# Sample-token attention scores issued in two halves around a third of a projection, and six unread matmuls at the end of the attention phase

## The chip, the cores and the metric

The kernel runs on one core of a Trainium2 chip. The metric is the device time of one launch in microseconds (us); the median of the runs of the kernel before is 1272.56 us.

## What is computed

One layer of a decoder trunk for 1024 prompt tokens and 64 sample tokens (8 sequences of 8), model width 1024. Cut to what matters here:

```python
xn = rmsnorm(x, norm_attn_g)
a, b, q, k, v, ga, gb = split(xn @ w_in)             # a, b, ga, gb: 1024 columns each
glu = a * sigmoid(b)
conv_out = silu(layernorm(causal_depthwise_conv(glu, w_dw, width=31))) @ w_conv_out
s = q @ k.T / 8 + rel_bias;  p = softmax([s, sink])   # window of 128, 16 heads, 4 kv heads
attn_out = (p @ v) @ w_attn_out                        # sample tokens: 128 cached keys + 8 new
h = x + (sigmoid(ga) * conv_out + sigmoid(gb) * attn_out) @ w_out
y = h + hier_moe(rmsnorm(h))                           # top group, then 2 of its 8 experts
```

## The kernel before

Every large product is done as three float16 products (high by high, high by low, low by high: the helper `mm3`, lines 74 to 76), so its operands are cut into a high half by ScalarE and a low half by VectorE. The program has three phases, each a block in which the five engines run their own instruction streams and wait for each other on semaphores: `attention_phase` (q, k, v and the attention of the prompt tokens), `conv_phase` (the projections a, b, ga, gb, the convolution, and the attention of the sample tokens), `ffn_phase` (output projection, routing, experts). Between phases all engines meet (line 96 ends a block; `phase_end` clears the semaphores on GpSimd, line 2718, and has the engines meet again, line 2720).

The order in each engine's stream is written by hand. What bears on the change:

- **End of the attention phase.** TensorE's last work is `feature(16, 24)`, the last third of the first b projection (bank `c_psb`). Its last product raises `feat_mm`, which VectorE waits for at the end of its own block. The helper `keep_warm` (line 743) issues products of 512 columns into the bank `a_psP` that nobody reads; `last_tile` uses it in three places.
- **A product of `conv_phase`** (`product`) computes 128 output features for all 1092 token columns in three thirds of 364 columns, 24 products of 0.15 us each. The a projections go to the bank `c_psa`, b and ga to `c_psb`. `first_chunk` on TensorE goes: 20 small transposes of the sample q and k (`sample_turn`, lines 1593 and 1596), the a projection (product 1), `sample_scores` for four groups of heads (lines 1612, 1616, tiles of 32 columns), product 2 (ga) with the transposes of the sample probabilities (`sample_turn_probs`, line 1624) ahead of its last third, `sample_turn_new` (line 1631), product 3 with `sample_values` (1644, 1648) and `sample_turn_out` (1655) between its thirds.
- **Scores.** The four groups share two halves of the bank `c_psm`: group 2 overwrites group 0, so TensorE waits for VectorE's logits of groups 0 and 1 (`s_logit`).
- **VectorE** in the same stretch: the low halves of the sample operands and of two weight chunks (lines 1312 to 1326, 1288), then `chunk(0, 0)`, the gated product a times sigmoid(b) (lines 1301, 1304, waits through ScalarE's line 1072 for all of product 1), then `sample_softmax`, which begins with the logits of the four groups (line 1334, two a group) and ends in two small operations on the maxima (1341, 1345), then the weight cut `low(4, 0)` (1288), then `conv`: 29 taps of about 1.2 us (line 1396) into which other work is put by count. After the tap of j = 8 stand the low halves of the transposed probabilities (`sample_probs`, line 1360), after j = 10 those of the new keys' (1367).
- **ScalarE**: `glu_a` (1072), the first tap (1078), the weight cut `cut(4, 0)` (1062), the second tap (1087), eight exponentials of the sample softmax (1139), further cuts, the high halves of the transposed probabilities (1147).

`sample_turn_probs` waits for all eight exponentials (`s_exp`); `sample_turn_new` waits, bank half by bank half, for the low halves of line 1360 (`s_pT_low`), because it overwrites them.

Of the kernel before, what the change touches and what calls it, by code (L numbers as in the profile page):

```python
# [36 lines left out]
HD, NH, NKV = 64, 16, 4  # L37
# [34 lines left out]
def mm3(pe, out, stat, mov, start, stop):  # L72

    pe.matmul(out, stat[0], mov[0], start=start, stop=False)  # L74
    pe.matmul(out, stat[0], mov[1], start=False, stop=False)  # L75
    return pe.matmul(out, stat[1], mov[0], start=False, stop=stop)  # L76
# [17 lines left out]
def attention_phase(nc, sem, g, A):  # L94

    with ExitStack() as c:
# [524 lines left out]
        def _(pe):  # L621
# [146 lines left out]
            def feature(first, last):  # L768

                for i in range(first, last):  # L770
                    third, k = i // KC, i % KC
                    cols = slice(third * THIRD, (third + 1) * THIRD)
                    done = mm3(pe, g.psb[:, third, 0:THIRD], (g.f_w_h[:, 0, k], g.f_w_l[0][:, k]),
                               (g.xnT_h[:, k, cols], g.xnT_l[:, k, cols]), k == 0, k == KC - 1)
                if last == 3 * KC:
                    done.then_inc(feat_mm, 1)
# [63 lines left out]
            last.then_inc(T_done, 1)  # L840
            pe.wait_ge(s_free, 16 * NT)
            feature(16, 24)


def conv_phase(nc, sem, g, A):
# [3 lines left out]
    with ExitStack() as c:  # L849
# [39 lines left out]
        def take32(n):  # L889
# [24 lines left out]
        s_q_low, s_kn_low, s_kT_low, s_v_low, s_vn_low = (sem("s_" + n) for n in (  # L914
            "q_low", "kn_low", "kT_low", "v_low", "vn_low"))
# [51 lines left out]
        def slot32(n):  # L967
            if isinstance(n, int):
                return w32[:, n % W32]
            return w32[:, ds(n % W32, 1)].rearrange("p a n -> p (a n)")  # L970
# [308 lines left out]
        def _(dve):  # L1279
# [6 lines left out]
            def low(n, pos):  # L1286
                dve.wait_ge(w_high, n + 1)
                dve.scalar_tensor_tensor(w_l[pos], slot32(n).rearrange("p (k m) -> p k m", k=KC), S_W,
                                         w_h[:, pos], op0=ALU.mult, op1=ALU.subtract).then_inc(w_low, 1)
# [7 lines left out]
            def chunk(k, p):  # L1297
                dve.wait_ge(th_done, k + 1)
                dve.wait_ge(a_out, k + 1)
                dve.wait_ge(hist_ld, 16 * k + 16)  # L1300
                dve.scalar_tensor_tensor(glu[:, p, HIST:HIST + SEQ], th[:, 0:SEQ], 1.0, a_s[:, 0:SEQ],
                                         op0=ALU.add, op1=ALU.mult).then_inc(glu_done, 1)
                seqs = glu[:, p, HIST + SEQ:].rearrange("p (b n) -> p b n", b=NSEQ)
                dve.scalar_tensor_tensor(seqs[:, :, HIST:], th[:, SEQ:T].rearrange("p (b i) -> p b i", b=NSEQ), 1.0,  # L1304
                                         a_s[:, SEQ:T].rearrange("p (b i) -> p b i", b=NSEQ),
                                         op0=ALU.add, op1=ALU.mult).then_inc(glu_done, 1)
# [19 lines left out]
                    dve.scalar_tensor_tensor(s_vn_l[:, h], g.v_s[HS * h:HS * h + HS, :], S_X, s_vn_h[:, h],  # L1326
                                             op0=ALU.mult, op1=ALU.subtract).then_inc(s_vn_low, 1)

            def sample_softmax():
                for grp in range(NKV):  # L1330
                    dve.wait_ge(s_mm, grp + 1)
                    for h in range(2):
                        u = 2 * grp + h
                        dve.tensor_tensor_reduce(s_p[:, u], ps_s[:, grp % 2, h], g.s_bias[:, grp], scale=1.0 / S_LOGIT,
                                                 scalar=NEG, op0=ALU.add, op1=ALU.max,
                                                 accum_out=s_st[:, 0, u:u + 1]).then_inc(s_logit, 1)
                dve.wait_ge(s_logit, SU)
                dve.sem_inc(s_stat, 1)
                dve.wait_ge(s_sink, 1)
                sink_b = g.s_nsink[:].unsqueeze(2).to_broadcast([P, NKV, 2])  # L1340
                dve.scalar_tensor_tensor(s_st[:, 1].rearrange("p (g h) -> p g h", h=2),
                                         s_st[:, 0].rearrange("p (g h) -> p g h", h=2), -1.0, sink_b, op0=ALU.mult,
                                         op1=ALU.min).then_inc(s_stat, 1)
                dve.wait_ge(s_stat, 2)
                dve.tensor_tensor(s_st[:, 2].rearrange("p (g h) -> p g h", h=2),
                                  s_st[:, 1].rearrange("p (g h) -> p g h", h=2), sink_b, ALU.subtract).then_inc(s_stat, 1)
                dve.memset(y[:, :, T:TM], 0.0).then_inc(setup, 1)
                dve.wait_ge(vec_ld, 16)
                dve.tensor_scalar(halves[:], vecs[:, 1:3], 0.5, None, ALU.mult).then_inc(setup, 1)
# [70 lines left out]

            sample_operands()
            low(3, 3)
            chunk(0, 0)
            sample_softmax()
            low(4, 0)
            dve.wait_ge(taps_ld, 16)
# [118 lines left out]
        def _(pe):  # L1545
# [41 lines left out]
            def half(j):  # L1587
                return slice(HD * (j // 2), HD * (j // 2) + HD)

            def sample_turn():  # L1590
                for h in range(NH):
                    out = ps_q[:, h // 8].rearrange("d b (h i) -> d b h i", h=8)[:, :, h % 8]
                    last = pe.transpose(out, g.q_s[0:TS, h * HD:(h + 1) * HD], g.ident[0:TS, 0:TS])
                last.then_inc(s_q_mm, 1)
                for grp in range(NKV):
                    last = pe.transpose(ps_k[:, grp // 2, grp % 2], g.k_s[0:TS, grp * HD:(grp + 1) * HD], g.ident[0:TS, 0:TS])
                last.then_inc(s_k_mm, 1)

            def sample_scores():
                pe.wait_ge(s_q_low, 2)  # L1600
                pe.wait_ge(s_kn_low, 2)
                pe.wait_ge(s_kT_low, 1)
                for grp in range(NKV):
                    r, heads = half(grp), slice(32 * (grp % 2), 32 * (grp % 2) + 32)
                    if grp > 1:
                        pe.wait_ge(s_logit, 2 * (grp - 1))
                    for h in range(2):
                        out = ps_s[:, grp % 2, h]
                        for i, (q, k) in enumerate(((s_qT_h, s_kT_h), (s_qT_h, s_kT_l), (s_qT_l, s_kT_h))):
                            for b4 in range(4):  # L1610
                                b = 4 * h + b4
                                pe.matmul(out[32 * b4:32 * b4 + 32, 0:WIN], q[r, b, heads],
                                          k[r, (grp % 2) * NSEQ + b, :], start=i == 0, stop=i == 2)
                        for i, (q, k) in enumerate(((s_qT_h, s_kn_h), (s_qT_h, s_kn_l), (s_qT_l, s_kn_h))):
                            for b4 in range(4):
                                last = pe.matmul(out[32 * b4:32 * b4 + 32, WIN:SW], q[r, 4 * h + b4, heads],
                                                 k[r, grp % 2, HS * h:HS * h + HS], start=i == 0, stop=i == 2)
                    last.then_inc(s_mm, 1)

            def sample_turn_probs():  # L1620
                pe.wait_ge(s_exp, SU)
                for bank in range(2):
                    for i in range(4):
                        last = pe.transpose(ps_t[:, bank, i], s_p[:, 4 * bank + i, 0:WIN], g.ident[:])
                    last.then_inc(s_pT_mm, 1)
# [32 lines left out]
            def keep_warm(n, bank, from_):  # L1658
                for i in range(n):
                    pe.matmul(bank, from_[:, i % KC, 0:P], from_[:, i % KC, 0:512], start=True, stop=True)  # L1660

            def first_chunk():
                pe.sem_inc(b_mm, 1)
                sample_turn()
                product(1, 1, psa, a_mm, xn, (0, 1))
                pe.wait_ge(s_kn_low, 2)
                product(1, 1, psa, a_mm, xn, (2,))
                sample_scores()
                pe.wait_ge(th_done, 1)
                product(2, 2, psb, ga_mm, xn, (0, 1))  # L1670
                sample_turn_probs()
                product(2, 2, psb, ga_mm, xn, (2,))
                sample_turn_new()
                pe.wait_ge(a_out, 1)
                product(3, 3, psa, ex_mm, xn, (0,))
                sample_values()
                product(3, 3, psa, ex_mm, xn, (1,))
                sample_turn_out()
                product(3, 3, psa, ex_mm, xn, (2,))

            def chunk(u, p, first=False):
# [14 lines left out]
                product(4 * k + 3, 3, psa, ex_mm, o if p else xn)  # L1696

            first_chunk()
            chunk(0, 1, True)
            with pe.Fori(1, KC // 2) as u:  # L1700
# [1153 lines left out]
```

## Time and profile before

| | |
|---|---|
| time, three runs | 1270.76, 1272.56, 1273.21 us (median 1272.56) |
| the profiled execution | 1273.04 us, of which the span of the trace 1271.4 us |
| TensorE busy | 1228.9 us (97%) |
| VectorE, ScalarE, GpSimd busy | 1036.4, 705.8, 311.5 us |
| mean granted clock of TensorE | 0.994 of full speed |
| attention phase, conv phase, ffn phase on TensorE | to 291.2, 292.8 to 842.6, from 843.9 us |

Times in the rows are us from the start of the span. A row of a timeline tells when an instruction (or a run of like ones) began and how long it lasted, and in brackets how long its engine had been idle before it and who ended that. Matmuls overlap in the pipe: a product of 364 columns is shown with 0.32 us but a new one begins every 0.15 us. A granted clock of 1.00 is 2.4 GHz, 0.50 is 1.2 GHz.

### The profile page before, as it was taken

To read this page: it belongs to the slowest core of one execution; us is meant where nothing else is said; L and a number is where in the kernel's file an instruction comes from. 1 tells how busy PE (TensorE), PEld (TensorE's weight loads), DVE (VectorE), ACT (ScalarE), POOL (GpSimd) and SP (SyncE) were. 2 spreads that over 40 slices of the span, in tenths; PEclk is the share of its full clock that TensorE was granted. 3 is DMA by queue.
4 is the path that set the end of the run, shared out by engine and by line. 5 is a ranking of instruction groups with operands and counts; after the bars stand their busy time and mean duration, and the time that the engine had idled before them with its cause. 6 is when DMAs were issued, how large, how long until landed. Compare 5 with 4: busy or idle time off the path is not lost. (4 is left out here: it accounts for less than half of the span.)

```text
span 1271.4 us, 28372 instructions
## 1 busy us (share of the span) xinstructions
PE 1228.9 (97%) x11174; PEld 821.8 (65%) x11174; DVE 1036.4 (82%) x1479; ACT 705.8 (56%) x1160; POOL 311.5 (25%) x280
## 2 busy tenths in 40 slices
PE   7899999998999999999999999999998999999995
PEld 5456666665666666666665666655555888888884
DVE  5777777776989999999999676535756999999993
ACT  5656666666443452354343664423222899999983
POOL 1383111111010010011000000000134367667663
PEclk9999999998999999999999999999999999999998
DMA  9700000033141442244141145547678999999982
GB/s 349 173 10 3 1 0 0 3 122 101 56 110 54 125 111 76 84 127 110 36 137 51 52 143 202 173 172 278 235 235 307 321 391 386 391 398 384 387 307 48
DMA packets 53081, 211.34 MB, mean 166 GB/s; under 512 B 14560, under 2 KB 15776, under 8 KB 40416
## 3 DMA queue, kind: packets, MB, share of 16 engines
q1 hardware_dynamic: 31888, 156.95, 33.1%
q0 software_dynamic: 18672, 44.42, 14.4%
q10 hardware_dynamic: 2448, 8.98, 1.8%
q8 instruction: 47, 0.77, 0.3%
q14 instruction: 26, 0.21, 0.1%
HBM read 180.98 MB, written 39.72 MB: 174 GB/s over the span
## 5 line engine op out<-in xcount | busy, mean ns | idle before, releaser
L1396 DVE SCALAR_TENSOR_TENSOR big<-c_region,c_taps,big 128x1024 f32<-128x1024 f32 (+1 forms) x120 | 153.4, 1279 | 3.7 <-ACT caT L1087 3.7
L74 PE MATMUL c_psb<-xnT,w_taken 128*128 128x364 f16 x456 | 145.5, 319 | 0.0
L75 PE MATMUL c_psb<-xnT,w_taken 128*128 128x364 f16 x456 | 145.5, 319 | 0.0
L1396 DVE SCALAR_TENSOR_TENSOR caT<-c_region,c_taps,caT 128x1024 f32<-128x1024 f32 x112 | 143.2, 1278 | 0.0
L2095 POOL DMA_INDIRECT y_all<-o_hn,e_idx_y x29 | 91.9, 3168 | 38.8 <-POOL e_idx_y L2091 23.3
L74 PE MATMUL c_psa<-xnT,w_taken 128*128 128x364 f16 x312 | 99.8, 320 | 0.1
L75 PE MATMUL c_psa<-xnT,w_taken 128*128 128x364 f16 x312 | 99.8, 320 | 0.0
L74 PE MATMUL o_psH<-big,e_gu 128*128 128x128 f16 x512 | 87.4, 219 | 0.8 <-DVE big L2442 0.8
L75 PE MATMUL o_psH<-big,e_gu 128*128 128x128 f16 x512 | 87.4, 219 | 0.0
L76 PE MATMUL o_psH<-big,e_gu 128*128 128x128 f16 x512 | 87.4, 219 | 0.0
L76 PE MATMUL c_psb<-xnT,f_w_l_first 128*128 128x364 f16 x240 | 76.2, 317 | 0.0
L353 ACT ACTIVATE big<-big,a_ntop 128x256 f32<-128x256 f32 (+1 forms) x128 | 61.4, 483 | 20.5 <-DVE a_ntop L505 20.5
L270 POOL TENSOR_TENSOR a_rs<-a_ms,neg_half 128x20 f32<-128x20 f32 x9 | 31.8, 3539 | 160.2 <-DVE a_ms L461 160.2
L76 PE MATMUL c_psb<-xnT,f_w_l 128*128 128x364 f16 x216 | 69.2, 320 | 0.0
L2431 DVE SCALAR_TENSOR_TENSOR e_gu<-e_gu 128x2048 f16<-128x2048 f32 x28 | 64.0, 2289 | 5.5 <-ACT e_gu L2157 5.5
L1018 POOL DMA_DIRECT2D sc_prompt<-c_region x8 | 4.6, 573 | 260.4 <-DVE c_region L1304 260.4
L74 PE MATMUL a_psP<-big,xnT 128*128 128x512 f16 x176 | 66.9, 380 | 0.0
L75 PE MATMUL a_psP<-w_taken,xnT 128*128 128x512 f16 x176 | 66.7, 379 | 0.0
L76 PE MATMUL a_psP<-big,xnT 128*128 128x512 f16 x176 | 66.7, 379 | 0.0
L74 PE MATMUL c_psa<-oT_h,w_taken 128*128 128x364 f16 x192 | 61.0, 318 | 1.2 <-ACT c_gate_b L1116 1.2
L76 PE MATMUL c_psa<-xnT,f_w_l_first 128*128 128x364 f16 x192 | 61.6, 321 | 0.0
L74 PEld LDWEIGHTS c_psb<-xnT,w_taken 128*128 128x128 f16 x456 | 44.9, 98 | 25.7 <-issue 0.3
(437 smaller groups left out, 3977.2 us busy)
## 6 DMA issues: line engine op xcount, KB each, us to landing
e_gu<-w_gu SPq DMA_DIRECT2D x28, 1024.0 KB, 12.0
w_taken<-w_feat SPq DMA_DIRECT2D x48, 512.0 KB, 4.1
e_d<-w_dn SPq DMA_DIRECT2D x15, 1024.0 KB
o_room<-w_gu SPq DMA_DIRECT2D x12, 1024.0 KB
xnT<-w_gu SPq DMA_DIRECT2D x12, 1024.0 KB
big<-w_gu SPq DMA_DIRECT2D x12, 1024.0 KB
c_region<-gates POOLq DMA_DIRECT2D x8, 1092.0 KB, 5.8
xnT<-w_dn SPq DMA_DIRECT2D x6, 1024.0 KB
```

The costliest lines, as they stand in the source:

```text
L74: pe.matmul(out, stat[0], mov[0], start=start, stop=False)
L75: pe.matmul(out, stat[0], mov[1], start=False, stop=False)
L76: return pe.matmul(out, stat[1], mov[0], start=False, stop=stop)
L270: pool.tensor_tensor(rs[:], ms[:], g.neg_half[:, 0:NH + NKV], ALU.pow).then_inc(rs_done, 1)
L353: act.activation(prob[:, s, r, lo:], prob[:, s, r, lo:], ACT.Exp, bias=ntop[:, s, r:r + 1], accum_out=den[:, s, r:r + 1]).then_inc(exp_don ...
L1018: pool.dma_start(A["sc_prompt"][ds(k * P, P), :], glu[:, p, SEQ:SEQ + HIST].rearrange("p a n -> p (a n)")).then_inc(hist_ps, 16)
L1396: dve.scalar_tensor_tensor(y_j, glu[:, p, j:j + SEQ], tap, y_j, op0=ALU.mult, op1=ALU.add).then_inc(tap_done, 1)
L2095: pool.indirect_dma_start(out=A["y_all"], out_offset=bass.IndirectOffsetOnAxis(ap=idx_y[:, p:p + 1], axis=0), in_=y_o[:, p], in_offset=Non ...
L2431: dve.scalar_tensor_tensor(gu_l[:, p, halves[half]], gu32[load[0]][:, halves[half]], S_W, gu_h[:, p, halves[half]], op0=ALU.mult, op1=ALU. ...
```

## The change

TensorE scores groups 0 and 1 after two thirds of product 1, then does the last third, then scores groups 2 and 3. VectorE does the logits of groups 0 and 1 before `chunk(0, 0)` and those of groups 2 and 3 behind it. At the end of the attention phase TensorE issues six unread products of 512 columns.

```diff
@@ attention_phase, TensorE
             pe.wait_ge(s_free, 16 * NT)
             feature(16, 24)
+            keep_warm(6)
@@ conv_phase, VectorE
-            def sample_softmax():
-                for grp in range(NKV):
+            def sample_logits(groups):
+                for grp in groups:
                     dve.wait_ge(s_mm, grp + 1)
                     for h in range(2):
                         u = 2 * grp + h
                         dve.tensor_tensor_reduce(s_p[:, u], ps_s[:, grp % 2, h], g.s_bias[:, grp], scale=1.0 / S_LOGIT,
                                                  scalar=NEG, op0=ALU.add, op1=ALU.max,
                                                  accum_out=s_st[:, 0, u:u + 1]).then_inc(s_logit, 1)
+
+            def sample_softmax():
                 dve.wait_ge(s_logit, SU)
@@
             sample_operands()
             low(3, 3)
+            sample_logits((0, 1))
             chunk(0, 0)
+            sample_logits((2, 3))
             sample_softmax()
             low(4, 0)
@@ conv_phase, TensorE
-            def sample_scores():
-                pe.wait_ge(s_q_low, 2)
-                pe.wait_ge(s_kn_low, 2)
-                pe.wait_ge(s_kT_low, 1)
-                for grp in range(NKV):
+            def sample_scores(groups):
+                if 0 in groups:
+                    pe.wait_ge(s_q_low, 2)
+                    pe.wait_ge(s_kn_low, 2)
+                    pe.wait_ge(s_kT_low, 1)
+                for grp in groups:
                     r, heads = half(grp), slice(32 * (grp % 2), 32 * (grp % 2) + 32)
                     if grp > 1:
                         pe.wait_ge(s_logit, 2 * (grp - 1))
@@
                 product(1, 1, psa, a_mm, xn, (0, 1))
-                pe.wait_ge(s_kn_low, 2)
+                sample_scores((0, 1))
                 product(1, 1, psa, a_mm, xn, (2,))
-                sample_scores()
+                sample_scores((2, 3))
                 pe.wait_ge(th_done, 1)
```

The order of the instructions on VectorE around `chunk(0, 0)` (lines 1301 and 1304 before, 1302 and 1305 with the change), before:

```order
L1304 SCALAR_TENSOR_TENSOR c_region<-c_region 128x8x8
L1334 ISA caT<-c_psm,big 128x160
L1334 ISA caT 128x1
L1334 ISA caT<-c_psm,big 128x160
L1334 ISA caT 128x1
L1334 ISA caT<-c_psm,big 128x160
L1334 ISA caT 128x1
L1334 ISA caT<-c_psm,big 128x160
L1334 ISA caT 128x1
L1334 ISA caT<-c_psm,big 128x160
L1334 ISA caT 128x1
```

and with the change:

```order
L1289 SCALAR_TENSOR_TENSOR f_w_l<-w_taken 128x1024
L1335 ISA caT<-c_psm,big 128x160
L1335 ISA caT 128x1
L1335 ISA caT<-c_psm,big 128x160
L1335 ISA caT 128x1
L1335 ISA caT<-c_psm,big 128x160
L1335 ISA caT 128x1
L1335 ISA caT<-c_psm,big 128x160
L1335 ISA caT 128x1
L1302 SCALAR_TENSOR_TENSOR c_region<-c_region 128x1024
L1305 SCALAR_TENSOR_TENSOR c_region<-c_region 128x8x8
L1335 ISA caT<-c_psm,big 128x160
```

Each logit is a pair of rows. All eight pairs stood behind `chunk(0, 0)`; now four stand ahead of it and four behind. The taps and what stands between them keep their order.

On TensorE, from the end of product 1 (`c_psa`) through the scores (lines 1612 and 1616 before, 1618 and 1622 with the change) to product 2 (`c_psb`), before:

```order
L76 MATMUL c_psa<-xnT,f_w_l_first 128x364
L1612 MATMUL c_psm<-caT 32x128 x12
L1616 MATMUL c_psm<-caT 32x32 x12
L1612 MATMUL c_psm<-caT 32x128 x12
L1616 MATMUL c_psm<-caT 32x32 x12
```

and with the change, from two thirds of product 1 into its last third:

```order
L76 MATMUL c_psa<-xnT,f_w_l_first 128x364
L1618 MATMUL c_psm<-caT 32x128 x12
L1622 MATMUL c_psm<-caT 32x32 x12
L1618 MATMUL c_psm<-caT 32x128 x12
L1622 MATMUL c_psm<-caT 32x32 x12
L1618 MATMUL c_psm<-caT 32x128 x12
L1622 MATMUL c_psm<-caT 32x32 x12
L1618 MATMUL c_psm<-caT 32x128 x12
L1622 MATMUL c_psm<-caT 32x32 x12
L74 MATMUL c_psa<-xnT,w_taken 128x364
```

Eight such pairs stood behind all of product 1; four of them now stand ahead of its last third, the other four behind it.

## Rows read from the trace of the kernel before

**Rows 1.** The page, busy time and share of each engine.

```profile
PE 1228.9 (97%) x11174; PEld 821.8 (65%) x11174; DVE 1036.4 (82%) x1479; ACT 705.8 (56%) x1160; POOL 311.5 (25%) x280
```

**Rows 2.** Waits of TensorE, whole span: us in total, times, longest.

```profile
PE c_psm L1612 <- DVE caT L1334: 2.0, 1, 2.0
PE c_psm L1593 <- PEq L2720: 1.6, 1, 1.6
PE c_psm L1566 <- DVE big L1419: 0.7, 1, 0.7
```

**Rows 3.** Timeline of TensorE around the end of the attention phase.

```profile
290.88 0.32 PE L76 MATMUL c_psb<-xnT,f_w_l_first 128*128 128x364 f16 x1
...
292.79 1.05 PE L1593 MATMUL c_psm<-ident,c_gate 64*64 64x64 f32 x16 [1.59 <-PEq L2720]
...
294.00 0.47 PE L74 MATMUL c_psa<-xnT,w_taken 128*128 128x364 f16 x1
```

**Rows 4.** Windows: length, busy of each engine, TensorE's clock (third last), DMA share, GB/s.

```profile
294.00:294.10 0.10, 0.10 (x3) 0.10 (x2) 0.00 (x0) 0.10 (x1) 0.06 (x1) 0.69 0.72 248
297.40:297.50 0.10, 0.10 (x2) 0.05 (x1) 0.00 (x0) 0.10 (x1) 0.00 (x0) 0.75 0.73 246
311.10:311.20 0.10, 0.10 (x17) 0.07 (x3) 0.10 (x3) 0.10 (x1) 0.10 (x1) 0.52 0.16 29
314.50:314.60 0.10, 0.10 (x2) 0.09 (x1) 0.10 (x1) 0.10 (x1) 0.00 (x0) 0.92 0.00 0
```

**Rows 5.** Timeline of TensorE around the end of the conv phase.

```profile
839.42 3.18 PE L1660 MATMUL c_psa<-caT 128*128 128x512 f16 x14
...
843.89 0.38 PE L74 MATMUL o_psH<-xnT,big 128*128 128x512 f16 x1 [1.29 <-PEq L2720]
```

**Rows 6.** Windows around two other idle stretches of TensorE: one, and after each.

```profile
56.99:58.80 1.81, 0.00 (x1) 0.03 (x1) 1.81 (x3) 0.60 (x1) 0.00 (x0) 1.00 0.56 127
58.80:62.20 3.40, 2.36 (x14) 1.38 (x14) 3.32 (x5) 1.94 (x3) 0.00 (x0) 1.00 0.49 92
843.89:847.50 3.61, 3.61 (x17) 1.66 (x18) 0.23 (x2) 0.00 (x0) 0.15 (x1) 1.00 0.59 210
```

**Rows 7.** Timeline of TensorE around the sample scores.

```profile
306.87 0.35 PE L1612 MATMUL c_psm<-caT 64*32 64x128 f16 x12
...
310.06 0.35 PE L1612 MATMUL c_psm<-caT 64*32 64x128 f16 x12 [2.04 <-DVE caT L1334]
...
311.14 0.49 PE L74 MATMUL c_psb<-xnT,w_taken 128*128 128x364 f16 x1
```

**Rows 8.** Timeline of VectorE, from the last low half to the weight cut.

```profile
304.25 1.22 DVE L1288 SCALAR_TENSOR_TENSOR f_w_l<-w_taken 128x1024 f16<-128x1024 f32 x1
308.16 1.23 DVE L1301 SCALAR_TENSOR_TENSOR c_region<-c_region 128x1024 f32<-128x1024 f32 x1 [2.68 <-issue]
...
309.44 0.32 DVE L1334 CUSTOM_DVE_ANT_0 caT<-c_psm,big 128x160 f32<-128x160 f32 x1
...
312.39 1.22 DVE L1288 SCALAR_TENSOR_TENSOR f_w_l_first<-w_taken 128x1024 f16<-128x1024 f32 x1
```

**Rows 9.** Timeline of ScalarE: a projection out, weight cut, last exponential.

```profile
306.98 1.08 ACT L1072 ACTIVATE c_region<-c_psa 128x1092 f32<-128x1092 f32 x1 [4.62 <-PE c_psa L76]
...
310.72 1.04 ACT L1062 ACTIVATE w_taken<-w_taken 128x1024 f16<-128x1024 f32 x1
...
315.91 0.19 ACT L1139 ACTIVATION_READ_ACCUMULATOR caT<-caT 128x1 f32 x1
```

**Rows 10.** Timeline of TensorE around the last third of product 2.

```profile
320.19 1.04 PE L1624 MATMUL c_psm<-ident,caT 128*128 128x128 f32 x8
321.07 0.32 PE L74 MATMUL c_psb<-xnT,w_taken 128*128 128x364 f16 x1
...
324.77 1.04 PE L1631 MATMUL c_psm<-ident,caT 128*32 128x128 f32 x8
325.64 0.32 PE L74 MATMUL c_psa<-xnT,w_taken 128*128 128x364 f16 x1
```

**Rows 11.** Timeline of VectorE: the low halves that `sample_turn_new` waits for.

```profile
323.03 1.28 DVE L1360 SCALAR_TENSOR_TENSOR caT<-c_psm,caT 128x512 f16<-128x512 f32 x2
```

**Rows 12.** Timeline of VectorE: its wait for the second chunk.

```profile
364.48 1.22 DVE L1301 SCALAR_TENSOR_TENSOR c_region<-c_region 128x1024 f32<-128x1024 f32 x1 [4.83 <-issue]
```

## The prediction

> **What bounds the kernel now.** I read the busy shares first [rows 1]: TensorE is busy 97% of the span, so a change pays only by what it takes out of TensorE's stream, as idle time or as time at the low clock. Then the waits of TensorE [rows 2]: the longest two in the stretch of the change are 2.0 us on VectorE's logits and 1.6 us on the meeting of the engines between the phases. From the scores to the end of the convolution it has only one other, 0.7 us, on VectorE's last sum. Then the granted clock [rows 4]: it goes to 0.50 twice here, from 294.0 to 297.45 and from 311.1 to 314.5, some 3.4 us each. Half speed for 3.4 us of dense products costs 1.7 us. The first fall comes after the idle time at the phase boundary and 1.2 us of 64-column transposes [rows 3], the second after the 2.04 us of idle time between narrow score products [rows 7]. So about 2.0 + 1.6 + 1.7 + 1.7 = 7 us are at stake, and the question is how much of that the edit takes out of the path.
>
> **The six unread products.** Fourteen of them last 3.18 us, the last one 0.38 [rows 5], so one begins every 2.80 / 13 = 0.215 us, and six put TensorE's last end off by 1.29 us. Nothing hides that: VectorE's stream ends by its wait for the product just ahead of them, and all engines meet behind. What comes back: at the end of the conv phase, where such products stand last on TensorE and VectorE has finished a little before, the gap from TensorE's last end to its next start is 1.29 us [rows 5], where the boundary in question has 1.59 [rows 3], because there VectorE only begins to leave when TensorE is done. I take that 0.3 us back: **+1.0 us**, between +1.0 and +1.3. The products stand ahead of the gap, not in it: an idle stretch of about 1.3 us and the 1.2 us of transposes still follow.
>
> **The scores in halves.** Half of the scores take 311.14 - 310.06 = 1.08 us [rows 7]. The first half now stands ahead of product 1's last third, at about 303.1 (306.8 less a third of 3.7 us, the length from 321.07 to 324.77 [rows 10]). The operands are there: VectorE is past them at 304.25, where it is at the last weight cut [rows 8]. So everything that waits for the whole of product 1 comes 1.08 us later: ScalarE's line 1072 at 308.06 instead of 306.98 [rows 9], the gated product at 309.24 instead of 308.16. The four logits ahead of it cost nothing: VectorE idles 2.68 us there [rows 8], and four take about 1 us. The wait of 2.04 us is gone, as logits 0 and 1 are done by about 306.5 and TensorE wants to overwrite them at 308.06. It begins product 2 at 308.06 + 1.08 = 309.14, where it was 311.14 [rows 7], and does two thirds at full clock in 7.4 us: 316.54, against 320.19 [rows 10]. **Up to here TensorE has gained 3.65 us**, 2.0 by the wait and 1.65 by the second fall.
>
> **What is late next.** First the exponentials. They end at 316.10 [rows 9], and their chain on ScalarE begins with line 1072, so now at 317.2. TensorE stands 0.65 us, then does the transposes (0.88 us) and the last third (3.70 us) [rows 10] and is ready for `sample_turn_new` at 321.8. Second, and this decides, that step waits for the low halves that VectorE makes after its tap of j = 8 [rows 11]. VectorE's place is set by ScalarE: `cut(4, 0)` ended at 311.76 [rows 9] and now ends at 312.84, so `low(4, 0)` cannot begin at 312.39 [rows 8] but at about 312.9, 0.5 us later than before, though its logits were partly done early. All taps follow 0.5 us late. The first pair half is ready at 323.03 + 0.68 + 0.5 = 324.2, the second at 324.8. TensorE was never waiting there: it came at 324.77, 0.46 us after VectorE was done. Now it stands from 321.8 to 324.2, **2.4 us**, does four transposes, waits for the second half and goes on with product 3 at about 324.85 + 0.44 = 325.3 instead of 325.64 [rows 10]. Of the 3.65 us gained 0.35 are left. Behind it nothing else is late: the next low halves and the norm come with the taps 3 and 10 us further on, where TensorE's stream has dense thirds between, and at the second chunk VectorE has 4.83 us of slack [rows 12], so from there both go at TensorE's pace and the shift is carried to the end.
>
> Sum with the clock left aside: +1.0 - 0.35 = **+0.65 us**. The second fall is in it already (it costs 324.8 to 325.64, less than 1.7, since without it TensorE would have met the same wait on VectorE).
>
> **The clock.** Two idle stretches matter. The one at the boundary, 1.3 us idle plus 1.2 us of narrow transposes, is now 2.5 us of little work instead of 2.8. The new wait is 2.4 us between dense products. No row shows either. On one side stand 1.81 us of idle time between dense products [rows 6] and 1.29 us [rows 5, 6] after which the clock stayed at 1.00; on the other 1.59 us with transposes and 2.04 us between narrow products, which ended in a fall [rows 3, 4, 7]. Both new ones lie between, each may fall or hold. If the first holds, 1.7 us come back; if the new wait makes one, up to 1.7 us are lost, less where part of the low stretch lies in the wait itself. I take about even chances for each, so the likeliest single outcome is that one of the two falls is there: +0.65.
>
> The profiled execution took 1273.04 us, 0.5 above the median of the runs. The sum gives 1273.7 against it, 1273.2 against the median. I forecast **1273.3 us**.
>
> **Rivals.**
> 1. *Both fall* (slower). TensorE stands at `sample_turn_new`, the clock goes to half in the first third of product 3, and the one after the boundary stays: +0.65 + 1.7 = +2.35, 1274.9; with the unread products at their full 1.3 us 1275.2 (0.2% above before). For it: 2.4 us is longer than every idle stretch of this trace after which the clock held, and longer than the two before a fall. Against it: both sides of it are dense. It decides from the point where the low clock falls wholly behind the wait. The Trainium skill has a rule on its side, on the page "TensorE: Matmul & The Clock Gate", section "A second HAM failure mode: psum-queue depth-cycling": a TensorE that idles briefly between groups of matmuls again and again lets its clock swing between the levels. By that rule the two new waits would cost the clock; the trace agrees for the 2.04 us wait, not for the 1.81 us one.
> 2. *Neither falls.* The unread products carry TensorE over the boundary and the new wait is too short: +0.65 - 1.7 = -1.05, 1271.5.
> 3. *VectorE is not late.* If my placing of line 1360 is wrong, the 3.65 us stay: +1.0 - 3.65 = -2.65, 1269.9, and 1268.2 with the first fall gone as well. For it: VectorE idled 2.68 us and has work moved into that. Against it: ScalarE's chain, which sets VectorE's restart, gets later, not earlier.
> 4. *The products do not do what their name says*: the gap follows them and the clock falls as before. That is inside the forecast and rival 1.
>
> **How the numbers follow.** One of two falls 0.42, both 0.25, neither 0.20, VectorE not late 0.13. A measurement of this kernel can tell about 0.2%, 2.5 us, from no change. Slower by more than that is a good half of rival 1 and a little beside it: 0.16. Faster by more is rival 3 and the edge of rival 2: 0.15. Within: 0.69. The range leaves out most of rival 3 and the far end of rival 1: 1270.2 to 1275.6.
>
> **What would show it.** In the changed trace: line 743 six times at 291; a gap of about 1.3 us behind; product 1's last third between two halves of the scores, with no wait at either; a wait of 0.6 us before line 1630 (the transposes of the probabilities) and one of 2.4 us before line 1637 (`sample_turn_new`) on VectorE's low halves, which come 0.5 us later from the phase's start. The phase's first transpose should come 1.0 us later than before, and product 3 should begin 0.65 us later than before with one fall of the clock. No wait at line 1637 would make the prediction wrong on the fast side; any other long wait in the first chunk, or a low clock for more than 7 us in all, on the slow side.

## The result, and the profile after

22 runs of each kernel: the changed kernel 1273.93 us on the median (1271.69 to 1276.45), the kernel before 1272.64 us (1270.61 to 1276.38). The ratio is 1.0014, with a 95% interval from 1.0007 to 1.0020: 0.9 to 2.5 us slower, which is clear of zero and within 0.2%. The time was forecast at 1273.3 us. The executions of the kernel before lie in two groups, 7 at 1270.6 to 1271.4 us and 14 at 1272.2 to 1273.5 (one took 1276.4), so the 1.29 us between the medians depend on how the groups are mixed. The profiled execution of before, 1273.04 us, is of the longer kind.

The page of the profiled execution (1274.4 us) and TensorE's waits in it, in us in total, times, longest:

```profile
span 1272.8 us, 28383 instructions
PE 1229.0 (97%) x11180; PEld 821.2 (65%) x11180; DVE 1036.5 (81%) x1479; ACT 705.9 (55%) x1160; POOL 310.0 (24%) x280
```

```profile
PE c_psm L1637 <- DVE caT L1363: 2.3, 1, 2.3
PE c_psm L1598 <- PEq L2726: 1.4, 1, 1.4
PE c_psm L1630 <- ACT caT L1140: 0.6, 1, 0.6
PE c_psa L76 <- issue: 0.4, 1, 0.4
```

TensorE is as busy as before [rows 1]. The wait of 2.0 us at the scores [rows 2] is gone, and two others stand in its place: 0.6 us before the transposes of the probabilities (line 1630), on the exponentials, and 2.3 us before those of the new probabilities (line 1637), on VectorE's low halves. The last row is new at this place: 0.4 us of idle time inside product 3 that waits for nothing the profile shows ("issue").

The timeline of TensorE, where [rows 3], [rows 7] and [rows 10] were:

```profile
290.37 0.32 PE L76 MATMUL c_psb<-xnT,f_w_l_first 128*128 128x364 f16 x1
...
293.34 1.05 PE L1598 MATMUL c_psm<-ident,c_gate 64*64 64x64 f32 x16 [1.35 <-PEq L2726]
...
306.93 0.35 PE L1618 MATMUL c_psm<-caT 64*32 64x128 f16 x12
...
316.20 1.09 PE L1630 MATMUL c_psm<-ident,caT 128*128 128x128 f32 x8 [0.62 <-ACT caT L1140]
...
323.25 1.49 PE L1637 MATMUL c_psm<-ident,caT 128*32 128x128 f32 x8 [2.26 <-DVE caT L1363]
324.54 0.51 PE L74 MATMUL c_psa<-xnT,w_taken 128*128 128x364 f16 x1
```

and windows of it, TensorE's granted clock being the third number from the end:

```profile
294.00:297.50 3.50, 3.50 (x31) 2.34 (x30) 2.05 (x4) 3.37 (x6) 0.61 (x1) 1.00 0.65 137
324.00:324.50 0.50, 0.50 (x4) 0.37 (x3) 0.50 (x1) 0.49 (x1) 0.00 (x0) 0.54 0.00 0
327.00:327.50 0.50, 0.50 (x3) 0.26 (x2) 0.50 (x2) 0.00 (x0) 0.00 (x0) 0.55 0.58 227
```

Behind the boundary the clock held in this execution, and it fell once, from 324.0 to 327.3, behind the new wait. VectorE's side, in place of [rows 8] and [rows 11]: the weight cut waits for ScalarE's, and the low halves follow from it.

```profile
308.21 1.23 DVE L1302 SCALAR_TENSOR_TENSOR c_region<-c_region 128x1024 f32<-128x1024 f32 x1 [1.21 <-issue]
...
311.85 1.22 DVE L1289 SCALAR_TENSOR_TENSOR f_w_l_first<-w_taken 128x1024 f16<-128x1024 f32 x1 [0.46 <-ACT w_taken L1063]
...
322.51 1.28 DVE L1363 SCALAR_TENSOR_TENSOR caT<-c_psm,caT 128x512 f16<-128x512 f32 x2
```

Where the time went, profile against profile:

| stretch on TensorE | before | after | longer by |
|---|---|---|---|
| last useful product of the attention phase to the first transpose | 290.88 to 292.79 | 290.37 to 293.34 | +1.06 |
| to product 3 | to 325.64 | to 324.54 | -1.65 |
| first third of product 3, to the sample values | to 329.44 | to 329.77 | +1.43 |
| values and second third, to the output transposes | to 336.33 | to 337.24 | +0.58 |

Each row begins where the one above it ends. The sum is +1.42 us. The -1.65 has the fall behind the boundary in it, which before has and this execution has not. Outside of the table the attention phase was 0.51 us shorter in this execution, the way from the output transposes to the unread products at the end of the conv phase takes 503.1 us in both, and the ffn phase was 0.5 us longer, which makes up the 1.4 us between the spans.

### The profile page after: what moved, and what is told of

Its sections match the earlier page's. It is cut to its first block and busy times, and to the rows that moved or that the text cites. A ratio compares the mean times of both kernels' runs of the same rounds, so it can differ in the third digit from the quotient of the medians.

```text
span 1272.8 us, 28383 instructions
## 1 busy us (share of the span) xinstructions
PE 1229.0 (97%) x11180; PEld 821.2 (65%) x11180; DVE 1036.5 (81%) x1479; ACT 705.9 (55%) x1160; POOL 310.0 (24%) x280
```

## The experiments

They were timed beside the kernel before in three batches on three chips: e1 to e4, e5 to e8, e9 to e11. Each has a ratio to before within its batch, with a 95% interval in brackets; it comes from all executions of the two and is not the quotient of two medians. The median of before differs between the batches (1270.94, 1271.84, 1271.68 us), its mean hardly (1271.65, 1271.70, 1271.75).

For every execution of these batches the record has the mean granted clock over the span. Profiles with two falls of the clock in the first 50 us of the conv phase have 0.994 (before, e1, e8, e10), those with one 0.995 or 0.996 (after, e2, e5, e6, e11), those with none 0.996 or 0.997 (e3, e4, e7, e9). An estimate agrees: one fall costs 1.7 us of 1271, or 0.0013. Of the 90 executions of before in the batches 38 have 0.994, with a median of 1272.8 us, and 52 have more, with a median of 1270.7. So a profile is one draw out of several, and what it shows of the clock is compared with this number below.

**e1, the scores alone.**

```diff
             feature(16, 24)
-            keep_warm(6)
```

> The kernel before with the scores in halves and without the six unread products. My theory (VectorE's low halves of the probabilities decide, the scores' own gain of 3.65 us is given back at sample_turn_new): within 0.7 us of before on the median (1272.0 to 1273.3), the wait of 2.0 us at the scores gone, a wait of about 2.3 us before the transposes of the new probabilities. The rival that the halves are worth their 2 to 3.7 us and the unread products take it back: 1269 to 1270.5, no new wait.

Measured: 1272.61 us, ratio 1.0008 [0.9998, 1.0019]. TensorE's waits:

```profile
PE c_psm L1636 <- DVE caT L1362: 2.3, 1, 2.3
PE c_psm L1597 <- PEq L2725: 1.6, 1, 1.6
PE c_psm L1629 <- ACT caT L1139: 0.6, 1, 0.6
```

The halves by themselves gain nothing, and the new wait is there without the unread products. The rival that they are worth 2 to 3.7 us is out: the interval ends at a gain of 0.3 us. Its centre is 1.0 us slower, more than the 0.7 I had allowed. In this profile both falls are there, the one behind the boundary and one behind the new wait (325.1 to 328.5). From the first transpose to product 3 it takes 32.90 us against 32.85 before, and to the sample values 38.1 against 36.65.

**e2, the six products alone.** The kernel before with `keep_warm(6)` behind `feature(16, 24)`.

> The kernel before with the six unread products alone. My theory (they stand ahead of the idle stretch, lengthen the path by 1.29 us and give 0.3 back in the meeting of the engines): 1.0 us slower than before, 1273.6, where the clock falls as often as before; the gap behind them 1.3 us instead of 1.6. The rival that they keep the clock up: as fast as before or up to 0.7 us faster, with no low clock behind the boundary.

Measured: 1273.87 us, ratio 1.0015 [1.0006, 1.0024], 0.8 to 3.0 us slower.

```profile
290.40 1.46 PE L743 MATMUL a_psP<-xnT 128*128 128x512 f16 x6
293.22 1.05 PE L1594 MATMUL c_psm<-ident,c_gate 64*64 64x64 f32 x16 [1.35 <-PEq L2721]
```

The gap behind them is 1.35 us, as forecast, and they are on the path. They alone give a change of the size of the whole one. Its profile has the clock up behind the boundary and down behind the scores, and an idle time of 0.4 us on "issue" in product 3. But that execution took 1272.54 us at a mean clock of 0.995, and 7 of the 11 have 0.994, the value of profiles with two falls, with a median of 1273.9 us. So most executions of e2 seem to have one fall more than the profile; where it lies, no trace shows. The rival, as fast as before or faster, is out by the time.

**e3, the low halves two taps earlier.** The changed kernel with

```diff
-                    if first and j == 8:
+                    if first and j == 6:
                         sample_probs()
-                    if first and j == 10:
+                    if first and j == 8:
                         sample_new_probs()
```

> The changed kernel with VectorE's low halves of the probabilities after the tap j = 6 instead of 8, and those of the new keys after 8 instead of 10. My theory: the wait before the transposes of the new probabilities shrinks from 2.3 us to under 0.5, the fall of the clock behind it goes with it, 1270.5 to 1271.5 against 1273.9 of the changed kernel, so faster than before by 1 to 2 us. The rival that something else holds the first chunk (ScalarE, the second chunk's start): no change, 1273.9, with the wait turning up elsewhere.

Measured: 1270.36 us, ratio 0.9996 [0.9988, 1.0005], where the changed kernel has 1.0014. TensorE then:

```profile
315.78 1.09 PE L1630 MATMUL c_psm<-ident,caT 128*128 128x128 f32 x8 [0.63 <-ACT caT L1140]
320.44 1.21 PE L1637 MATMUL c_psm<-ident,caT 128*32 128x128 f32 x8
```

```profile
291.00:340.00 49.00, 46.62 (x664) 30.29 (x663) 42.25 (x67) 27.08 (x57) 3.37 (x4) 1.00 0.31 91
```

The wait of 2.3 us is gone, no low clock is left in the whole stretch, and the two intervals do not overlap (0.9988 to 1.0005 against 1.0007 to 1.0020), if barely, and from different batches. So the place of VectorE's low halves was what held the gain back. The time in microseconds is as forecast, but "faster than before by 1 to 2 us" is not shown: by the ratio it is 0.5 us faster, from 1.5 faster to 0.6 slower.

**e4, TensorE takes the new probabilities a third later.** The changed kernel with

```diff
-                sample_turn_new()
                 pe.wait_ge(a_out, 1)
                 product(3, 3, psa, ex_mm, xn, (0,))
-                sample_values()
+                sample_turn_new()
                 product(3, 3, psa, ex_mm, xn, (1,))
-                sample_turn_out()
+                sample_values()
                 product(3, 3, psa, ex_mm, xn, (2,))
+                sample_turn_out()
```

> The changed kernel with the transposes of the new probabilities, the sample values and the output transposes each put off by one third of product 3 on TensorE, VectorE's order untouched. My theory: TensorE has 3.7 us of products to do while VectorE makes the low halves, the wait of 2.3 us goes, 1270.5 to 1271.5. The rival that VectorE then waits for TensorE (norm after j = 14, output after j = 18) and hands the delay on: slower than that, 1272.5 or more, with idle time on VectorE ahead of lines 1377 and 1384.

Measured: 1271.84 us, ratio 1.0000 [0.9991, 1.0009]. The wait on the low halves is gone here too, and no low clock is left in the profile. VectorE waited 1.06 us for the sample values and 0.79 us at the output, but together that is no more than in after (0.6 and 1.4 us), so these waits do not speak for the rival. TensorE idled on "issue":

```profile
PE c_psm L1650 <- issue: 0.8, 1, 0.8
```

By its ratio it stands between after and e3, and its interval overlaps with both, so it is told apart from neither. Why it is above my 1271.5 stays open; in the profile product 3 ends 44.6 us behind the first transpose, as in e3.

**e5, e3 without the unread products.**

> Scores in halves, low halves of the probabilities two taps earlier, no unread products. My theory: 1.1 us less than e3 by the boundary, and 0.4 to 0.6 us less if the unexplained idle time of TensorE in the thirds of product 3 (0.3 to 0.8 us, seen in every kernel with the products and in none without) goes with them; more often a fall of the clock behind the boundary costs 1.7 us again. So 1268.8 to 1270.5, and in the profile no issue gap before the sample values. The rival that the products earn their place by the clock: 1271.5 or more, slower than e3.

Measured: 1269.35 us, ratio 0.9984 [0.9975, 0.9993], 0.9 to 3.2 us faster than before, and the first version that beats it. TensorE's waits:

```profile
PE c_psm L1597 <- PEq L2725: 1.6, 1, 1.6
PE c_psm L1629 <- ACT caT L1139: 0.6, 1, 0.6
PE c_psm L1660 <- DVE caT L1376: 0.6, 1, 0.6
```

Its time is in the forecast range, but its interval overlaps with that of e3, so that it is faster than e3 is not shown. No issue gap, and one fall of the clock behind the boundary (293.5 to 297). From the first transpose to the output transposes it takes 41.6 us against 43.5 before.

**e6, the early low halves alone (control).**

> The kernel before with only the low halves two taps earlier (control). My theory: TensorE came 0.5 us after VectorE at that point, so nothing waits on it: within 0.3 us of before, and the wait of 2.0 us at the scores and its fall of the clock remain. The rival that the earlier low halves are worth something by themselves: 1 us or more faster.

Measured: 1271.03 us, ratio 0.9999 [0.9990, 1.0008]. As forecast nothing; the wait at the scores (2.0 us) and the low clock behind it are there. Together with the split scores they pay (e5).

**e7, unread products in the new wait.** e1 with

```diff
-                sample_turn_new()
                 pe.wait_ge(a_out, 1)
+                keep_warm(8, psa[:, 0], g.xnT_h)
+                sample_turn_new()
```

> Scores in halves without the boundary products (e1), with 8 unread products of 512 columns put into the new wait of 2.3 us ahead of the transposes of the new probabilities (1.7 us of work where TensorE stood anyway). My theory: they cost nothing and keep the clock at 1.00 behind the wait, so 1.0 to 1.7 us less than those runs of e1 that had that fall: median 1271 to 1271.7, and the low stretch at 325 to 328 us gone. The rival that the fall depends on more than this idle stretch: it stays, 1272.6 as e1.

Measured: 1272.22 us, ratio 1.0003 [0.9994, 1.0012]: not told apart from e1, and above the median I had given. The profile shows what they do:

```profile
320.80 1.89 PE L1665 MATMUL c_psa<-xnT 128*128 128x512 f16 x8
323.23 1.21 PE L1636 MATMUL c_psm<-ident,caT 128*32 128x128 f32 x8 [0.54 <-DVE caT L1362]
```

```profile
324.00:328.00 4.00, 4.00 (x28) 2.49 (x26) 4.00 (x5) 2.01 (x3) 0.00 (x0) 1.00 0.28 111
```

They cost no time, since TensorE still waits 0.54 us behind them, and the clock stays up where it fell in after and in e1. The other executions agree: their mean clock is 0.9962, that of e1 0.9950, a difference of one fall. An issue gap of 0.4 us came with them, which puts the products behind it off by 0.55 us.

**e8, twelve products.** `keep_warm(12)` in the place of six, otherwise before.

> The kernel before with twelve unread products at the end of the attention phase. My theory: they lie in full on the path, so 6 x 0.215 = 1.3 us more than e2, the gap behind them still 1.35 us: 1.0 + 1.3 = 2.3 us over before, with a fall of the clock as often as in e2. The rival that more of them keep the clock up: the fall behind the boundary never seen, and the time not above e2.

Measured: 1275.94 us, ratio 1.0032 [1.0020, 1.0044], 2.5 to 5.6 us slower.

```profile
290.51 2.75 PE L743 MATMUL a_psP<-xnT 128*128 128x512 f16 x12
294.62 1.05 PE L1594 MATMUL c_psm<-ident,c_gate 64*64 64x64 f32 x16 [1.35 <-PEq L2721]
```

```profile
PE c_psm L1649 <- issue: 0.9, 1, 0.9
```

From the last useful product to the first transpose it takes 4.27 us, where e2 takes 2.97, with the same gap of 1.35 us: the six more products lie on the path in full. On top of the 2.3 us expected the profile has 0.9 us on "issue", in the sample values, and a low clock right behind it (334.0 to 337.8) that no other profile has there. In e4, with 0.8 us on "issue" in the sample values, none followed, so that the gap set off the fall is not shown.

**e9, the six products in exchange for six others.** e2, with six of twelve unread products of the last tile taken away:

```diff
-                keep_warm(12)
+                keep_warm(6)
```

> e2 (the six unread products at the end of the attention phase) with six of the twelve unread products of the last tile taken away, so that TensorE's stream from the conv phase on holds the same instructions at the same places as before. My theory of the issue gap (0.3 to 0.9 us of idle time inside product 3 that waits for nothing, seen in all six kernels with instructions added to TensorE's stream and in none of the four without): it hangs on where the instructions lie, so here it is gone, while the 1.0 us of the boundary stays; how the last tile takes the loss is not forecast, up to 1.3 us either way in the attention phase. The rival that the gap comes with the products' work or time at the boundary: it is there as in e2, 0.4 us.

Measured: 1270.74 us, ratio 1.0000 [0.9991, 1.0009]. The issue gap is gone:

```profile
PE c_psm L1613 <- DVE caT L1335: 2.0, 1, 2.0
PE c_psm L1594 <- PEq L2721: 1.4, 1, 1.4
PE c_psm L1632 <- DVE caT L1361: 0.5, 1, 0.5
```

There was no low clock from 290 to 342 us in this execution, although the wait of 2.0 us between the scores is there, and TensorE met VectorE before the new probabilities (0.5 us, line 1632) even with the scores in one piece. The boundary takes 2.96 us, as long as in e2. The last tile of the attention phase seems to have made up for it, as the whole is not slower and the last useful product comes at 289.54 us instead of 290.88; that part was not taken apart.

**e10, one product.** `keep_warm(1)`, otherwise before.

> The kernel before with a single unread product at the boundary. By the place of the instructions: the issue gap of 0.3 to 0.9 us appears already here, though only 0.215 us of work is added. By the work: no gap. In both the gap of the boundary is 1.35 to 1.6 us and the whole is within 0.7 us of before.

Measured: 1270.63 us, ratio 0.9993 [0.9984, 1.0002]. No issue gap, and the clock fell twice, as in before. So one added product does not make the gap; six or more, net, did each time. This profile too is one draw: the mean clock of the 11 executions is 0.9962, and 0.9949 for before beside it.

**e11, the norm earlier too.** e5 with `if first and j == 14:` made `j == 12`.

> e5 with the norm of the sample output after the tap j = 12 instead of 14. In e5 TensorE stood 0.6 us there (line 1660 on VectorE's line 1376). If that wait is on the path like the others: 0.6 us less than e5 on the median. If the next wait takes its place: the same as e5.

Measured: 1270.18 us, ratio 0.9984 [0.9975, 0.9993]. The wait of 0.6 us before the output transposes is gone and that stretch takes 40.9 us in the profile, 0.7 less than in e5, with one fall behind the boundary in both. The time does not show it: the ratio is that of e5. I take it as no difference that can be measured.

## Why the prediction was right

The direction, the place of the new waits and their causes came as worked out. The size came out at about twice the +0.65 us of the sum, which lies just below the interval of 0.9 to 2.5 us, and that the time of 1273.3 us was so near is in part luck: about as much as was forecast came from an idle gap that the working did not have.

- **The six unread products: +1.0 forecast, +1.06 measured.** The gap behind them shrank from 1.59 to 1.35 us, 0.24 instead of the 0.3 taken. e2 and e8 show them on the path one for one.
- **The scores in halves.** TensorE stood at neither half. Up to the end of two thirds of product 2 the gain is 3.49 us (3.65 forecast; 27.40 us from the first transpose in before, 23.91 in e1, both with a fall behind the boundary). Then it waits 0.62 us at the probabilities (0.65 forecast) and 2.26 us at the new ones (2.4 forecast), and VectorE's weight cut is held up 0.46 us by ScalarE's (0.5 forecast). At product 3 nothing of the gain is left in e1, and 0.2 us in e7, where no fall follows the wait (30.96 us from the first transpose, 31.17 in e6, neither with a fall behind the boundary); 0.35 was forecast. e3, e5 and e6 show together that the low halves held the gain back: moved earlier they are worth nothing alone and the split nothing alone, and the two together without the unread products 0.9 to 3.2 us.
- **The second fall in before cost half of its 1.7 us**, as said: e2 and e6, which have this fall alone, take 31.2 us from the first transpose to product 3, and e9 without any 30.36, as TensorE runs into the wait on VectorE there instead. That is 0.8 us, as in the forecast (324.8 to 325.64).
- **The fall behind the new wait** costs its 1.7 us in full: in after and e1 it makes the transposes of the new probabilities 0.3 us longer than in e7 (1.49 and 1.52 against 1.21) and the first third of product 3 1.4 us longer than in before. It came in both profiles that have the wait, and the other executions agree: where the wait is, the mean clock is lower by 0.0010 (0.9955 in after, 0.9965 in e3) and by 0.0016 (0.9950 in e1, 0.9966 in e5), about the 0.0013 of one fall. The even chance that I gave it was too low. Behind the new wait of 0.62 us none came.
- **The fall behind the boundary.** It is missing in all six profiles with six or more unread products (after, e2, e3, e4, e8, e9), and there in five of seven with none or one (not in e6 and e7). So the profile has one of two falls, as in the forecast, and 19 of the 22 executions of after have a mean clock of 0.995 or 0.996, the values of profiles with one. But that the products keep the clock up is not shown beyond the profiled executions. Their counterparts without products have no lower clock: before 0.9949 and e2 0.9945, e5 0.9966 and e3 0.9965; only e1 and after, 0.9950 and 0.9955, go the way of the profiles. Nor do the products pay for their 1.06 us in any of these pairs: e2 is 1.9 us behind before by its ratio, e3 1.5 us behind e5, after 0.8 us behind e1, of which the first alone is clear of its interval. So rival 4, that they do not do what their name says, is not refuted.
- **What the sum did not have** is the issue gap. It was put at nothing, and the row of the table with +0.58 is that gap: 0.41 us of idle time, and 0.57 us in the starts of the products on its two sides (0.72 us instead of 0.15). With it the sum is 1.2 us, against 1.29 between the medians, 1.42 between the profiles and 1.8 by the ratio. No row of before could show it.
- **Rival 3, VectorE not late**, is out by the row of line 1637. Rival 1, both falls, is what e1's profile has, not after's.
- **A row misread.** From the scores to the end of the convolution the trace of before has not one other wait of TensorE but two: besides the 0.7 us there are 1.2 us on ScalarE's line 1116, between 640 and 700 us. Both stand in after as well, so nothing hangs on it.

## What to carry to other kernels

A wait taken out of the bounding engine pays only up to the next place where that engine meets a slower chain, so walk down from it to the next two waits before counting: here 3.5 us shrank to nothing within 14 us of program, and moving that next meeting point by two taps on VectorE, with the unread products left out, turned a loss of 0.14% into a gain of 0.16%. Unread products cost their full length when they stand ahead of a meeting of all engines (e2, e8), and nothing where the engine would wait anyway (e7). Whether they hold a clock up is to be read from many executions: one profile of each kernel said yes at the boundary, and the mean clocks of all executions did not. Count instructions added to a long unrolled stream as a possible cost of their own.

## What the runs showed that was not expected

**An idle gap that waits for nothing.** Six kernels had more instructions in TensorE's stream than before by six or more (after, e2, e3, e4, e7, e8), and each has an idle time on "issue" of 0.3 to 0.9 us in or next to product 3, as here in after:

```profile
334.30 0.33 PE L76 MATMUL c_psa<-xnT,f_w_l 128*128 128x364 f16 x1 [0.41 <-issue]
```

The seven with none or one more, or with six added and six taken away, have none there (before, e1, e5, e6, e9, e10, e11). e9 is the telling one: the same six products at the boundary, but the stream behind them at its old places, and no gap. So it goes with where the instructions lie, not with the work of the products.

A count makes this sharper. In all six kernels 3341 or 3342 matmuls lie ahead of the gap, though it stands at different points of the program: after five products of the second third of product 3 in after and e3, after four in e2, after three in e7, and inside the sample values in e4 and e8. Windows from the start of the span into the gap, of after and e8, with TensorE's matmuls in the first brackets:

```profile
0.00:334.10 334.10, 312.26 (x3342) 197.99 (x3342) 252.21 (x636) 200.37 (x473) 71.62 (x83) 0.99 0.25 76
0.00:333.20 333.20, 311.88 (x3341) 198.77 (x3342) 250.52 (x632) 200.53 (x473) 71.49 (x83) 0.99 0.25 76
```

But the count is not enough by itself, as before passes it at 334.3 us without a gap. A late fetch of instructions would fit; that was not tested, and where between one and six products it sets in stays open.

Nor is this the only idle time of the kind. The trace of before has a longer one in the ffn phase, where after waits 0.6 us for VectorE (line 2586):

```profile
PE o_psM L2580 <- issue: 1.7, 1, 1.7
```

**The clock behind the boundary.** The idle stretch was 1.6 us without the products and 1.35 us with them, and the transposes behind it the same. The profiles have five falls in seven without them, or with one, and none in six with them. All executions together do not bear this out: 7 of 11 of e2 have the mean clock of profiles with two falls, and 6 of 11 of e5, without products, have 0.997 or 0.998, which no profile with a fall has. What decides whether the clock falls behind the boundary stays open.
